# ScalarE copies the query and key banks, VectorE rotates them in SBUF: a two-layer hybrid encoder trunk

## The chip, the cores and the metric

The kernel runs on one core of one Trainium2 chip. The metric is the device time of one execution in microseconds (us), median of three runs. A core has five engines with queues of their own: TensorE (PE in the profile) multiplies matrices and writes its results to PSUM, eight banks of 128 partitions x 512 float32; VectorE (DVE), ScalarE (ACT) and GpSimd (POOL) work on elements; SyncE (SP) issues most of the loads. SBUF is the on-chip memory that all of them share. Engines wait for each other on semaphores, and each works through its own queue strictly in order.

## The reference, cut to what matters

```python
for layer in range(2):
    xn = rms_norm(x, norm_mix[layer])
    proj = xn @ w_in[layer]                     # 256 x 1024 @ 1024 x 4096
    q, k, v, u, gates = split(proj)             # q, k: 256 x (4 heads x 2 halves x 64)
    q, k = rotary(q, positions), rotary(k, positions)
    a = diff_attention(q, k, v, lam)            # softmax 1 - lam * softmax 2, per head
    s = s5_bidirectional(u, ...)                # diagonal state space, both directions
    x = x + (gate0 * (a @ w0) + gate1 * (glu(s) @ w1)) @ w_out
    x = x + (swiglu(x) if layer == 0 else top-2-of-8 experts(x))
return rms_norm(x, norm_final)

def rotary(x, positions):                       # per group of 64 columns
    x1, x2 = x[..., :32], x[..., 32:]
    return concatenate([x1 * cos - x2 * sin, x2 * cos + x1 * sin], -1)
```

All data is float32, DEPTH is 2, SEQ is 256, D_MODEL is 1024.

## The kernel before, in words

The 256 tokens stand in two halves of 128 partitions (`th` 0 and 1). Every weight matrix arrives in tiles of 128 x 2048 float32 (1 MB) in the slots of `raw`. A tile is split into two parts: ScalarE copies it rounded into `hi` (`split`, L1215), VectorE subtracts (`lo` = `raw` - `hi`, L1637, both inputs in SBUF), and TensorE multiplies hi by hi, hi by lo and lo by hi (`three`, L657). `hi` and `lo` have three slots, so tile t can be split once tile t-3 has been used.

A mixer (one per layer) first projects u, v, q and k (`W_IN_ORDER`), two tiles each: q is tiles 4 and 5, k is tiles 6 and 7. A projection writes both halves of tokens into two banks, `PJ[0]` and `PJ[1]`, 12 matmuls of 512 columns for each half and tile, and the next projection may write a bank when its reader has signalled `pj_free[th]`. u and v are read out of the banks by ScalarE (`from_pj`, L1266: a copy that multiplies by the inverse root of the norm). q and k are read by VectorE (`rotary`, L1687): for each half two products with the sine table into `areg` (L1700), one product with the cosine table in place in the bank (L1705), the sum into `qk` (L1706) and a memset that signals the bank free (L1708).

After k's projection TensorE transposes q (L675), computes the kernel of the state-space mixer inside a chunk (`inner`, L767 and L776), transposes k, and transposes the powers of the input matrix (eight turns, `B_TURNS`; ScalarE takes each out of its bank, L1253). `inner` waits for `b_part` and `kdiag_ready` from VectorE and for `c_ready` from GpSimd. The loop over eight scores and eight state-space steps follows.

The orders are written out by hand. VectorE's in the mixer of layer 0, from the sixth tile:

```python
split_static(t + 6)
rotary(l, "q", qk[:, 0, :, :])
split_static(t + 7)
input_power(b_power(3), 3)
input_power(b_power(4), 4)
# two memsets that signal b_part and b_ready
inner_diagonal(l)
rotary(l, "k", qk[:, 1, :, :])
split_static(t + 8)
split_static(t + 9)
```

In layer 1 VectorE has splits 6, then q, splits 7 and 8, then k, split 9; the input powers are GpSimd's there and are made earlier, during the feed-forward part. GpSimd in layer 0 works, in this stretch, through `c_chain` (three `product`s of 128 x 512 elements, L443 to L449, then the memset L2231 that signals `c_ready`), `phasors` (L464 to L467) and `phase_products` (L423, L2253, L2254), from which ScalarE makes the first scan table (`scan_tables`, L1326 and L1332) in the middle of the eight turns. Nearly all of these have both inputs in SBUF.

Of the kernel before, what the change touches and what calls it, by code (L numbers as in the profile page):

```python
# [18 lines left out]
P = 128  # L19
SEQ, D = 256, 1024  # L20
TH = SEQ // P
# [19 lines left out]
T_MIX = (0, T_MIX1)  # L41
# [82 lines left out]
def build(nc, x, norm_mix, w_in, attn_lambda, attn_subln, ssm_lam_re, ssm_lam_im, ssm_log_dt, ssm_b_re, ssm_b_im,  # L124
# [3 lines left out]
    ACT, ALU, AX = mybir.ActivationFunctionType, mybir.AluOpType, mybir.AxisListType  # L128
    MUL, ADD, SUB = ALU.mult, ALU.add, ALU.subtract
    ctx = ExitStack()  # L130
    with ctx:
# [3 lines left out]
        def sem(name):  # L135
            return ctx.enter_context(nc.semaphore(name))
# [10 lines left out]
        qk = sb("qk", [P, 2, TH, WA])  # L147
# [6 lines left out]
        small = sb("small", [P, 128])  # L154
# [15 lines left out]
        ident = cst[:, C_ID:C_ID + P]  # L170
# [53 lines left out]
        PJ, PY, PV, TR = banks[0:2], banks[2:4], banks[4:6], banks[6:8]  # L224

        raw_full = [sem(f"raw_full{i}") for i in range(RAWS)]
        hi_ready, lo_ready, tile_used = sem("hi_ready"), sem("lo_ready"), sem("tile_used")
        loads, x_in = sem("loads"), sem("x_in")
        rows_in, lam_in = sem("rows_in"), sem("lam_in")
# [8 lines left out]
        pj0_full = sem("pj0_full")  # L238
        pj_free = [sem("pj_free0"), sem("pj_free1")]
        dve_own, pool_own, act_own = sem("dve_own"), sem("pool_own"), sem("act_own")  # L240
        act_par, dve_par = sem("act_par"), sem("dve_par")
        rot_ready = sem("rot_ready")
# [56 lines left out]
        SS, VAR, RT, RI, MX, NB, RS, RR, C1 = 0, 2, 4, 6, 8, 10, 12, 14, 16  # L299
# [3 lines left out]
        def col(i, n=1):  # L303
            return small[:, i:i + n]
# [50 lines left out]
        def place_of(l, name):  # L355

            return W_IN_ORDER[l].index(name)

        def loop_tile(l):

            return T_MIX[l] + 16 - len(LOOP_PROJ[l])
# [6 lines left out]
        def use(l, i):  # L368

            return PJ_PER_LAYER * l + i  # L370

        def pj_read(l, i):

            return (PJ_PER_LAYER - 2) * l + i + 1
# [24 lines left out]
        place = vreg[:, 1, 0:256].rearrange("p (t s) -> p t s", t=2)  # L399
        dskip = small[:, 96:128].rearrange("p (l q) -> p l q", l=2)  # L400
        zero_mark = small[:, 92:93]
        root_mark = small[:, 22:23]
        ht_rows_hi = ht_hi[:, :, :].rearrange("p f s -> p (f s)").rearrange("p (f s) -> p f s", s=P)
        ht_rows_lo = ht_lo[:, :, :].rearrange("p f s -> p (f s)").rearrange("p (f s) -> p f s", s=P)
        gate_t = gate_store[:, :].rearrange("p (t c) -> p t c", t=TH)
# [2 lines left out]
        dve_mark, power_mark, bank_mark = small[:, 20:21], small[:, 21:22], small[:, 18:19]  # L408
# [799 lines left out]
        def _(act):  # L1208
            own = Order(act, act_own)
# [11 lines left out]
            def split_static(t):  # L1221
                s = raw_slot(t)
                split(t, raw_full[s], 32 * (raw_uses(s, t) + 1), raw[:, s, :], t % SPLITS, t >= SPLITS)
# [97 lines left out]
            def scan_tables(l, m):  # L1321
# [10 lines left out]
                    last = act.activation(lower, upper[:, :, ::-1], ACT.Copy, scale=1.0 if r == 0 else -1.0)  # L1332
                last.then_inc(wtab_ready, 1)

            def gate_block(l, name, tile, between=None):

                g, n = divmod(int(name[1]), 2)
                from_pj(l, place_of(l, name), tile, lambda th: gates[:, th, g, n * 512:(n + 1) * 512], ACT.Tanh,
                        lambda th: col(RH + th), between=between)

            def mixer(l):
# [40 lines left out]
                for g in range(2):  # L1382
                    evac((l, "u", g), ut4[:, 8 * g:8 * g + 8, :].rearrange("p q c -> p (q c)"))
                split_static(t + 6)
                split_static(t + 7)
                split_static(t + 8)
                for i in range(t + 9, loop_tile(l) + 2):
                    split_static(i)
                for th in range(TH):
# [12 lines left out]
                for s in range(8):  # L1402
# [12 lines left out]
                    if s == 7:  # L1415
                        tile, i, half = loop_proj(l, s)
                        gate_block(l, W_IN_ORDER[l][i], tile, lambda: (head_back(l, 6), weights_back(l, 7)))
                    elif s in LOOP_PROJ[l] and loop_proj(l, s)[2] == 1:
                        tile, i, half = loop_proj(l, s)
# [190 lines left out]
            for n in range(2):  # L1610
                for th in range(TH):
# [4 lines left out]
                    if n == 1:  # L1616
# [3 lines left out]
                                       scale=1.0 / D).then_inc(tail_root, 1)  # L1620
# [10 lines left out]
        def _(dve):  # L1631
            own = Order(dve, dve_own)
# [52 lines left out]
                    at_part(l, kind, 2 * th + n, 4 * n, 4, th * P, scale)  # L1685

            def rotary(l, name, dst):  # L1687
                i = place_of(l, name)

                cos_t = cst[:, C_COS:C_COS + HD].rearrange("p (t c) -> p t c", t=2)  # L1690
                sin_t = cst[:, C_SIN:C_SIN + P].rearrange("p (t c) -> p t c", t=2)
                for th in range(TH):
                    if th == 0:
                        dve.wait_ge(pj0_full, use(l, i) + 1)
                    else:
                        dve.wait_ge(tile_used, T_MIX[l] + 2 * i + 2)
                    src = PJ[th][:, :]
                    crossed = a_flat[:, 512 * th:512 * th + 512]
                    for a in range(2):
                        m = stt(crossed.rearrange("p (h a c) -> p h a c", a=2, c=32)[:, :, a, :],  # L1700
                                src.rearrange("p (h a c) -> p h a c", a=2, c=32)[:, :, 1 - a, :], col(RI + th),
                                sin_t[:, th, 32 * a:32 * (a + 1)].unsqueeze(1).broadcast_to([P, 8, 32]), MUL, MUL)
                    own.step(m)
                    halves = src.rearrange("p (h c) -> p h c", c=32)
                    own.step(stt(halves, halves, col(RI + th), cos_t[:, th, :].unsqueeze(1).broadcast_to([P, 16, 32]), MUL, MUL))  # L1705
                    tt(dst[:, th, :], src, crossed, ADD).then_inc(rot_ready, 1)  # L1706
                    dve.wait_ge(rot_ready, 4 * l + (0 if name == "q" else 2) + th + 1)
                    dve.memset(bank_mark, 0.0).then_inc(pj_free[th], 1)  # L1708

            def rotated(l, m):  # L1710

# [479 lines left out]
            for i, bank in enumerate(comb_banks):  # L2191
                n, th = i // 2, i % 2
# [228 lines left out]
```

## Time and profile before

| what | value |
|---|---|
| median of three runs | 1412.39 us (1411.92 to 1412.68) |
| the profiled execution's own time | 1413.66 us |
| its span, first to last instruction | 1410.4 us |
| TensorE busy | 1372.8 us (97% of the span) |
| VectorE busy | 1103.8 us (78%) |
| ScalarE busy | 895.5 us (63%) |
| GpSimd busy | 362.8 us (26%) |

Busy time is summed over a whole span that has very different stages: two mixers of about 250 and 190 us, a dense feed-forward part and the experts. The parts that the change touches lie at 60 to 90 us (layer 0) and 455 to 485 us (layer 1). Starts are given in us from the span's start, durations in us. Matmuls overlap each other, so their spacing (start to start) says more than their duration.

### The profile page before, as it was taken

What the parts mean: (1) busy time and instruction counts of PE and PEld (TensorE: products, weight loads), DVE (VectorE), ACT (ScalarE), POOL (GpSimd) and SP (SyncE); (2) the same over time, 40 slices, a digit from 0 to 9 for tenths busy, and PEclk for the clock granted to TensorE, in tenths of its full rate; (3) what the DMA queues carried; (4) which work ended last, traced back from release to release, by engine and by line L of the source; (5) the groups of instructions that cost most, each with busy time, mean ns of one, the idle gap of its engine ahead of it and who ended that gap; (6) DMA issues with size and microseconds to landing.
All of it is one profiled execution on the core that took longest, in us unless ns stands there. A gap on an engine that the chain in (4) does not pass through costs nothing.

```text
span 1410.4 us, 23374 instructions
## 1 busy us (share of the span) xinstructions
PE 1372.8 (97%) x8481; PEld 1123.9 (80%) x8481; DVE 1103.8 (78%) x1024; ACT 895.5 (63%) x905; POOL 362.8 (26%) x467
## 2 busy tenths in 40 slices
PE   6989999999999999999999999999999999999996
PEld 4778777888888788788888888888888888888885
DVE  6887677655455577678888888888888888898886
ACT  5445646444445455556777777777777777777775
POOL 6989709995000187000000000000000000000100
PEclk9999999999999999999999999999999999999999
DMA  9433355665555242697999999999999999999991
GB/s 244 160 121 116 116 169 166 208 197 189 184 174 180 71 156 91 243 327 282 371 370 369 389 374 379 387 359 387 384 367 389 376 376 386 367 385 350 385 349 30
DMA packets 194803, 385.12 MB, mean 273 GB/s; under 512 B 17969, under 2 KB 57265, under 8 KB 194610
## 3 DMA queue, kind: packets, MB, share of 16 engines
q1 hardware_dynamic: 188256, 367.48, 73.0%
q0 software_dynamic: 4336, 14.17, 3.9%
q10 hardware_dynamic: 2146, 2.59, 0.6%
q8 instruction: 42, 0.69, 0.2%
q14 instruction: 23, 0.19, 0.0%
HBM read 375.80 MB, written 7.34 MB: 272 GB/s over the span
## 4 chain that ended last, share of the span: by engine, by line
PE 88%; DVE 5%; ACT 3%; issue 2%; POOL 1%; DMA 0%; ACTq 0%; DVEq 0%; POOLq 0%
PE bank L657 84%; DVE lo L1637 2%; ACT hi L1215 1%; PE bank L1109 1%; PE bank L675 1%; PE bank L776 1%; POOL raw L2272 1%; PE bank L1092 0%; DVE raw L1756 0%; DVE bank L1758 0%; PE bank L983 0%; ACT at_hi L1544 0%; DMA areg<-in_norm_mix_dram 0%; PE bank L814 0%; ACT raw L1308 0%
## 5 line engine op out<-in xcount | busy, mean ns | idle before, releaser
L1637 DVE TENSOR_TENSOR lo<-raw,hi 128x2048 fp32r<-128x2048 f32 x347 | 802.5, 2324 | 156.1 <-ACT hi L1215 155.4
L1215 ACT ACTIVATE hi<-raw 128x2048 fp32r<-128x2048 f32 x347 | 663.7, 1916 | 181.5 <-PE bank L657 172.8
L657 PE MATMUL bank<-hi,at_hi 128*128 128x512 f32 x1288 | 513.9, 399 | 11.2 <-DVE lo L1637 5.8
L657 PE MATMUL bank<-hi,at_lo 128*128 128x512 f32 x1288 | 504.1, 391 | 0.0
L657 PE MATMUL bank<-lo,at_hi 128*128 128x512 f32 x1288 | 503.2, 391 | 0.0
L657 PEld LDWEIGHTS bank<-hi,at_hi 128*128 128x128 f32 x1288 | 242.9, 189 | 65.7 <-DVE lo L1637 10.8
L657 PEld LDWEIGHTS bank<-hi,at_lo 128*128 128x128 f32 x1288 | 242.6, 188 | 52.2
L657 PEld LDWEIGHTS bank<-lo,at_hi 128*128 128x128 f32 x1288 | 243.0, 189 | 47.5
L657 PE MATMUL bank<-hi,ht_hi 128*128 128x512 f32 x432 | 168.8, 391 | 0.9 <-DVE ht_lo L2115 0.9
L657 PE MATMUL bank<-hi,ht_lo 128*128 128x512 f32 x432 | 168.2, 389 | 0.0
L657 PE MATMUL bank<-lo,ht_hi 128*128 128x512 f32 x432 | 168.1, 389 | 0.0
L2348 POOL TENSOR_TENSOR small<-cst 128x1 f32<-128x1 f32 x14 | 5.9, 424 | 590.7 <-DVE slot_row L2152 298.6
L657 PEld LDWEIGHTS bank<-hi,ht_hi 128*128 128x128 f32 x432 | 81.1, 188 | 19.2 <-DVE lo L1637 1.5
L657 PEld LDWEIGHTS bank<-hi,ht_lo 128*128 128x128 f32 x432 | 81.1, 188 | 17.0
L657 PEld LDWEIGHTS bank<-lo,ht_hi 128*128 128x128 f32 x432 | 81.1, 188 | 16.6
L1553 ACT ACTIVATE ht_hi<-bank 128x512 fp32r<-128x512 f32 (+1 forms) x48 | 26.8, 559 | 55.7 <-PE bank L1109 55.7
L2272 POOL TENSOR_TENSOR raw<-raw 128x256 f32<-128x256 f32 x64 | 46.8, 761 | 22.3 <-ACT raw L1332 8.6
L1549 ACT ACTIVATE vreg<-bank 128x512 f32<-128x512 f32 (+1 forms) x48 | 27.1, 565 | 25.1 <-PE bank L657 25.1
L657 PEld LDWEIGHTS bank<-raw 64*64 64x64 f32 x1152 | 36.1, 134 | 8.0 <-issue 3.7
L657 PE MATMUL bank<-raw 64*64 64x64 f32 x1152 | 40.5, 221 | 0.3 <-POOL raw L2279 0.2
L2265 POOL MEMSET raw<- 128x4 f32 x4 | 0.3, 104 | 152.0 <-DVE raw L1733 152.0
L1227 ACT ACTIVATE at_hi<-bank 128x512 fp32r<-128x512 f32 x32 | 17.7, 596 | 33.5 <-PE bank L675 33.5
(308 smaller groups left out, 1152.7 us busy)
## 6 DMA issues: line engine op xcount, KB each, us to landing
raw<-in_moe_w_dram SPq DMA_DIRECT2D x528, 512.0 KB, 6.8
raw<-in_ffn_w_dram SPq DMA_DIRECT2D x66, 512.0 KB, 4.2
raw<-in_w_in_dram SPq DMA_DIRECT2D x64, 512.0 KB, 4.7
raw<-in_w_branch_dram SPq DMA_DIRECT2D x16, 512.0 KB, 4.5
raw<-in_w_out_dram SPq DMA_DIRECT2D x16, 512.0 KB, 4.7
raw<-in_w_glu_dram SPq DMA_DIRECT2D x4, 512.0 KB, 4.2
moe_sum<-xres POOLq DMA_DIRECT2D x3, 512.0 KB, 5.4
xres<-in_x_dram SPq DMA_DIRECT2D x2, 512.0 KB, 6.4
```

What stands on the lines that cost most here:

```text
L657: return pe.matmul(o, a, b, start=start, stop=stop)
L675: last = pe.transpose(bank[:, i * rows:(i + 1) * rows], src, ident[0:rows, 0:rows])
L776: m = pe.matmul(bank[r0:r0 + GC, c0:c0 + 64], bbar[rows, r, q, d, :], cblk[rows, r, q, 4 * d:4 * d + 4, :].rearrange("p i h -> p (i h)"), ...
L1109: m = pe.transpose(TR[0][:, f * P:(f + 1) * P], v_flat[:, f * P:(f + 1) * P], ident)
L1215: act.activation(hi[:, slot, :], src, ACT.Copy).then_inc(hi_ready, 1)
L1227: act.activation(at_hi[:, k0:k0 + kn, c0:c0 + P], bank[:, 0:kn * P].rearrange("p (k c) -> p k c", k=kn), ACT.Copy, scale=scale).then_inc(a ...
L1549: act.activation(v_flat[:, 0:h_width(c)], PJ[0][:, 0:h_width(c)], ACT.Silu).then_inc(g_ready, 1)
L1553: act.activation(ht_rows_hi[:, 0:h_width(c) // P, :], TR[0][:, 0:h_width(c)].rearrange("p (f s) -> p f s", s=P), ACT.Copy).then_inc(ht_hi_ ...
L1637: tt(lo[:, slot, :], src, hi[:, slot, :].bitcast(f32), SUB).then_inc(lo_ready, 1)
L2265: pool.memset(edge[:, :, :, 0:1], 0.0)
L2272: last = tt(dst, src[:, :, :, d, :], w[:, r:r + 1, :, d, :].broadcast_to([P, 2, 2, 64]), MUL)
L2348: tt(small[:, 82 + i:83 + i], ident[:, 0:1], ident[:, 0:1], MUL).then_inc(pool_passed, 1)
```

## The change

ScalarE gets `keep_rows`: for each half it copies the bank of q (or k), times the inverse root, into `qk`, signals `pj_free`, waits for that signal itself, and marks with a one-column activation that the rows are kept (`rows_kept`). VectorE's `rotary` waits for `rows_kept`, reads `qk` in place of the bank, uses `tensor_tensor` in place of `scalar_tensor_tensor`, and no longer signals the bank. `keep_rows` of q stands in ScalarE's queue after split 6, that of k after split 8.

```diff
+            def keep_rows(l, name, dst):
+
+                i = place_of(l, name)
+                for th in range(TH):
+                    if th == 0:
+                        act.wait_ge(pj0_full, use(l, i) + 1)
+                    else:
+                        act.wait_ge(tile_used, T_MIX[l] + 2 * i + 2)
+                    act.activation(dst[:, th, :], PJ[th][:, :], ACT.Copy, scale=inverse(th)).then_inc(pj_free[th], 1)
+                    act.wait_ge(pj_free[th], pj_read(l, i))
+                    act.activation(rows_mark, ident[:, 0:1], ACT.Copy).then_inc(rows_kept, 1)
...
                 split_static(t + 6)
+                keep_rows(l, "q", qk[:, 0, :, :])
                 split_static(t + 7)
                 split_static(t + 8)
+                keep_rows(l, "k", qk[:, 1, :, :])
...
             def rotary(l, name, dst):
-                i = place_of(l, name)
-
                 cos_t = cst[:, C_COS:C_COS + HD].rearrange("p (t c) -> p t c", t=2)
                 sin_t = cst[:, C_SIN:C_SIN + P].rearrange("p (t c) -> p t c", t=2)
                 for th in range(TH):
-                    if th == 0:
-                        dve.wait_ge(pj0_full, use(l, i) + 1)
-                    else:
-                        dve.wait_ge(tile_used, T_MIX[l] + 2 * i + 2)
-                    src = PJ[th][:, :]
+                    n = 4 * l + (0 if name == "q" else 2) + th + 1
+                    dve.wait_ge(rows_kept, n)
+                    src = dst[:, th, :]
                     crossed = a_flat[:, 512 * th:512 * th + 512]
                     for a in range(2):
-                        m = stt(crossed.rearrange("p (h a c) -> p h a c", a=2, c=32)[:, :, a, :],
-                                src.rearrange("p (h a c) -> p h a c", a=2, c=32)[:, :, 1 - a, :], col(RI + th),
-                                sin_t[:, th, 32 * a:32 * (a + 1)].unsqueeze(1).broadcast_to([P, 8, 32]), MUL, MUL)
+                        m = tt(crossed.rearrange("p (h a c) -> p h a c", a=2, c=32)[:, :, a, :],
+                               src.rearrange("p (h a c) -> p h a c", a=2, c=32)[:, :, 1 - a, :],
+                               sin_t[:, th, 32 * a:32 * (a + 1)].unsqueeze(1).broadcast_to([P, 8, 32]), MUL)
                     own.step(m)
-                    halves = src.rearrange("p (h c) -> p h c", c=32)
-                    own.step(stt(halves, halves, col(RI + th), cos_t[:, th, :].unsqueeze(1).broadcast_to([P, 16, 32]), MUL, MUL))
-                    tt(dst[:, th, :], src, crossed, ADD).then_inc(rot_ready, 1)
-                    dve.wait_ge(rot_ready, 4 * l + (0 if name == "q" else 2) + th + 1)
-                    dve.memset(bank_mark, 0.0).then_inc(pj_free[th], 1)
+                    parts = src.rearrange("p (h c) -> p h c", c=32)
+                    own.step(tt(parts, parts, cos_t[:, th, :].unsqueeze(1).broadcast_to([P, 16, 32]), MUL))
+                    tt(src, src, crossed, ADD).then_inc(rot_ready, 1)
```

## Rows read from the trace of the kernel before

**Rows 1.** The page: busy time of TensorE, and the last chain's shares by engine.
```profile
PE 1372.8 (97%) x8481; PEld 1123.9 (80%) x8481; DVE 1103.8 (78%) x1024; ACT 895.5 (63%) x905; POOL 362.8 (26%) x467
PE 88%; DVE 5%; ACT 3%; issue 2%; POOL 1%; DMA 0%; ACTq 0%; DVEq 0%; POOLq 0%
```

**Rows 2.** The chain of waits, 20 to 110 us: start, duration, what.
```profile
57.82 5.75 PE bank L657 x24
...
65.31 0.69 DVE qk L1706
...
68.59 1.28 DVE raw L1756 x2
...
76.64 0.44 DVE raw L1770
...
83.31 0.61 ACT qk L1476
...
84.05 8.68 PE bank L657 x288
```

**Rows 3.** VectorE in order of time, layer 0 (rotary halves, split 7).
```profile
63.60 0.88 DVE L1700 SCALAR_TENSOR_TENSOR areg<-bank,small,cst 128x256 f32<-128x256 f32 x2 [0.20 <-PE bank L657]
...
66.04 2.63 DVE L1637 TENSOR_TENSOR lo<-raw,hi 128x2048 fp32r<-128x2048 f32 x1
...
81.24 0.69 DVE L1706 TENSOR_TENSOR qk<-bank,areg 128x512 f32<-128x512 f32 x1
```

**Rows 4.** The chain of waits, 430 to 500 us, its longest piece.
```profile
430.00 39.41 PE bank L657 x291
```

**Rows 5.** ScalarE in order of time, layer 0.
```profile
49.20 0.69 ACT L1266 ACTIVATE vreg<-bank,small 128x512 f32<-128x512 f32 x1 [0.18 <-PE bank L657]
...
88.83 0.50 ACT L1332 ACTIVATE raw<-raw 128x128 f32<-128x128 f32 x2
...
94.67 0.21 ACT L1401 ACTIVATE small<-small 128x4 f32<-128x4 f32 x1
```

**Rows 6.** GpSimd in order of time: products beside VectorE's splits 5 and 6.
```profile
54.56 1.06 POOL L443 TENSOR_TENSOR raw<-raw,par 128x512 f32<-128x512 f32 x1
55.58 3.11 POOL L445 TENSOR_TENSOR raw<-raw,par 128x512 f32<-128x512 f32 x1
58.65 3.11 POOL L445 TENSOR_TENSOR raw<-raw,par 128x512 f32<-128x512 f32 x1
```

**Rows 7.** VectorE in order of time: splits 5 and 6 together, then split 6.
```profile
54.92 5.92 DVE L1637 TENSOR_TENSOR lo<-raw,hi 128x2048 fp32r<-128x2048 f32 x2
57.69 3.15 DVE L1637 TENSOR_TENSOR lo<-raw,hi 128x2048 fp32r<-128x2048 f32 x1
```

**Rows 8.** Groups of VectorE, 450 to 485 us (GpSimd idle): count, busy, mean ns.
```profile
L1637 DVE TENSOR_TENSOR lo<-raw,hi 128x2048 fp32r<-128x2048 f32 x4 | 9.1, 2288 | 5.3 <-ACT hi L1215 5.3
L1700 DVE SCALAR_TENSOR_TENSOR areg<-bank,small,cst 128x256 f32<-128x256 f32 x8 | 3.5, 480 | 5.5 <-PE bank L657 5.5
L1706 DVE TENSOR_TENSOR qk<-bank,areg 128x512 f32<-128x512 f32 x4 | 2.8, 692 | 0.1
```

**Rows 9.** Short instructions side by side: GpSimd, then VectorE.
```profile
28.85 0.77 POOL L2297 TENSOR_TENSOR gates<-gates 128x256 f32<-128x256 f32 x1
29.05 0.71 DVE L1997 TENSOR_TENSOR gates<-gates 64x128 f32<-64x128 f32 x1
```

**Rows 10.** GpSimd in order of time: beside rotary q, `c_ready`, the first phase table.
```profile
61.84 1.29 POOL L448 TENSOR_TENSOR raw<-raw 128x512 f32<-128x512 f32 x1
...
73.31 0.10 POOL L2231 MEMSET small<- 128x1 f32 x1
...
88.15 0.45 POOL L2254 TENSOR_TENSOR raw<-php_last 128x128 f32<-128x128 f32 x1
```

**Rows 11.** TensorE in order of time: after a pause; layer 1 around tiles 6 and 7.
```profile
33.64 0.47 PE L657 MATMUL bank<-hi,at_hi 128*128 128x512 f32 x1 [2.16 <-ACT ureg L1266]
...
35.07 0.63 PE L657 MATMUL bank<-hi,at_lo 128*128 128x512 f32 x1
...
458.26 0.47 PE L657 MATMUL bank<-hi,at_hi 128*128 128x512 f32 x1
...
463.81 0.39 PE L657 MATMUL bank<-hi,at_hi 128*128 128x512 f32 x1
```

**Rows 12.** TensorE by stretch: busy (count), granted clock, DMA share, GB/s.
```profile
36.00:38.00 2.00, 2.00 (x6) 0.50 1.04 370
```

More of the change, by code:

```diff
@@ L226, in build @@
         raw_full = [sem(f"raw_full{i}") for i in range(RAWS)]
+        rows_kept = sem("rows_kept")
         hi_ready, lo_ready, tile_used = sem("hi_ready"), sem("lo_ready"), sem("tile_used")
@@ L401, in build @@
         zero_mark = small[:, 92:93]
-        root_mark = small[:, 22:23]
+        root_mark, rows_mark = small[:, 22:23], small[:, 18:19]
         ht_rows_hi = ht_hi[:, :, :].rearrange("p f s -> p (f s)").rearrange("p (f s) -> p f s", s=P)
```

## The prediction

> **What bounds the kernel now.** I read the page's shares first: TensorE is busy 97% of the span and makes 88% of the chain that ended last [rows 1]. So a change to VectorE and ScalarE matters only where that chain leaves TensorE, and I went to the chain of waits at the two places that the diff touches.
>
> Layer 1 first, since it is simple: from 430 to 469.4 us the chain is one piece of TensorE [rows 4]. It is never left for a rotation there, and GpSimd is idle in that stretch. The rotations cost nothing today as long as they end in time.
>
> Layer 0 is different [rows 2]. TensorE's tile 5 ends at 63.57; from there the chain is on VectorE: the second half of q's rotation (last instruction 65.31 to 66.00), split 7, the input powers (68.59 on), the diagonal (76.64), and only at 77.33 TensorE's inner kernel. It ends at about 82.6; k's transposes, ScalarE's copy of them at 83.31 and the eight turns from 84.05 follow. In this stretch TensorE waits for VectorE, and a microsecond more on VectorE is a microsecond more on the run. k's rotation (81.24 to 81.93, [rows 3]) ends 0.7 us before k's transposes start: hardly any slack.
>
> **The third engine.** GpSimd's and VectorE's rows in one stretch show what the diff's words do not. GpSimd's products of 128x512 take 1.06 us [rows 6]; the two beside splits 5 and 6 took 3.11 each. The split takes 2.29 us when GpSimd is idle [rows 8], but here two took 5.92 and the second 3.15 [rows 7]. The ends fit one pattern. Product L443 ends at 55.62; 55.49 + 2.29 is 57.78, split 5's end. Product L445 ends at 58.69 = 57.63 + 1.06; 58.55 + 2.29 = 60.84, split 6's end. The next product ends at 61.76 = 60.70 + 1.06. So they take turns, one instruction each, every one starting 0.14 us before the recorded end of the other's. It holds for short ones too: a GpSimd product ends at 28.85 + 0.77 = 29.62, and VectorE's L1997 of 64x128, asked for at 29.05, ends at 29.76 [rows 9]. Counted back from there by the 0.28 us that its kind takes, it started at 29.48, again 0.14 before the product's end. VectorE instructions with one input in PSUM show none of this: L1700 has 0.88 for two beside busy GpSimd [rows 3] as in layer 1 (0.48 each, [rows 8]), and GpSimd's L448 beside them its plain 1.29 [rows 10].
>
> The change turns 16 such instructions with a PSUM input (four per half, four halves per mixer) into instructions with both inputs in SBUF. In layer 0 GpSimd is busy all through them.
>
> The Trainium skill (SBUF — State Buffer, Who interferes with whom) speaks against the change in the same way: a VectorE instruction with two SBUF inputs and a GpSimd instruction that reads SBUF exclude each other, and who issues first holds the port for the whole instruction. The rows agree but for the 0.14 us of overlap; taken literally it is a rival below.
>
> **Layer 0, step by step.** (1) Handoff. The ScalarE copy of a bank with a scale takes 0.69, the mark 0.21 [rows 5], waits 0.04 each: 0.98. It cannot be hidden for the second half, whose bank is full at 63.56. VectorE may start half 0 at 61.84 (before: 60.88), half 1 not before 64.54. The mark is bounded by 0.10 (a one-column memset, [rows 10]) and 0.50 (two activations of 128 columns, [rows 5]).
>
> (2) The rotation itself, without GpSimd: two sine products of 0.43 (0.05 less than the 0.48 of today), cosine and sum 0.69 each (as L1706) and waits: 2.25 a half, today 2.43. I see no faster form: 2288 ns for 2048 against 692 for 512 [rows 8] is 1.04 ns an element with SBUF inputs only, just what the PSUM ones have.
>
> (3) Taking turns with GpSimd, q. From 61.84 the products are L448, L449 (1.29 each), then L443, L443, L445, L445 (1.06), L448, L449. With each start at the other's end less 0.14: L448 to 63.13; sine 62.99-63.42; L449 to 64.57; sine 64.43-64.86; L443 to 65.78; cosine 65.64-66.33; L443 to 67.25; sum 67.11-67.80. Half 1: L445 to 68.72; sine to 69.01; L445 to 69.93; sine to 70.22; L448 to 71.37; cosine to 71.92; L449 to 73.07; sum 72.93-73.62. Today it ends at 66.00: +7.6. If VectorE wins the first turn (both ask at 61.84) every step comes one product earlier, 72.4: +6.4. With an overlap of 0.10 in place of 0.14 it is 74.2: +8.2.
>
> GpSimd loses little by it, since split 7 now falls later: `c_ready` comes at 73.2, as today (73.31, [rows 10]), long before it is needed.
>
> (4) Split 7 waits 0.3 for a product and ends at 76.27 (68.67 today). TensorE, which wants tile 7 at about 69.0, idles 7.3 us. That is not added: the inner kernel waits for VectorE anyway. From split 7's end to the diagonal's end VectorE needs 8.4 us as today (68.67 to 77.08): 84.70. +7.6, TensorE's inner kernel at 84.96.
>
> The pause has a clock price. After 2.16 us of idling at 31.5 us matmuls came 0.43 apart from 34.65 to 38.06 in place of 0.23, granted clock 0.50 (1.2 of 2.4 GHz) [rows 11, 12]: 8 of them, 1.6 us. Tile 7, from 76.32, needs 5.46 + about 1.9 and the q transposes 1.0 to 1.9: 84.7 to 85.6. Hidden, or 0.6 late.
>
> (5) k's rotation, from 84.72: the phase products (0.40 and 0.45 us) stand between now, 0.2 for each: 90.24, 5.5 us against 4.8. ScalarE's split 9 and q's copies come after the kept k (84.7 to 87.7), ahead of k's transposes. These start at 90.28 (the inner kernel ends at 90.26), the two inner copies of ScalarE, which wait for the rotation, end at 91.26, and k's copy starts at 91.26 in place of 83.31: **+7.95**. The first phase table (88.60 today, 88.3 then) and splits 8 and 9 (95.1) are early for what follows; everything behind is moved by the same amount, since loads and GpSimd's steps of the loop wait for this chain too.
>
> **Layer 1.** GpSimd is idle. ScalarE's split 7 (452.93 today) now stands behind the kept q, whose second half is full at 458.28: kept and marked 459.27, rotation to 461.5, VectorE's split 7 to 463.85. Tile 7 was taken at 463.81; tile 6 starts 0.2 sooner, because its bank is free at 456.3 and the pause before 458.26 goes [rows 11]. TensorE then waits some 0.3, net **+0.15** (bounds -0.22 and +0.5). k's rotation ends at 472.6, wanted at 475.
>
> **Sum.** 7.95 + 0.15 = 8.1 us. Against the profiled execution: 1413.66 + 8.1 = 1421.8 (span 1418.5). Its own time stands 1.27 above the median of the runs, so for the median 1412.39 + 8.1 = **1420.5**.
>
> **Rivals.**
> (a) VectorE has the right of way: its instructions are not held up, only GpSimd's. Then VectorE is 0.8 later, but GpSimd loses 2 x (0.29 + 0.55) = 1.7 per half, 6.7 over four halves, and the first phase table comes at 95.3, where ScalarE would take it at 88.83 + 0.8 [rows 5, 10] and holds back the turns behind it: +6.5. 1412.4 + 6.5 + 0.15 = 1419.0. For it: GpSimd lost most beside splits. Against: split 6's 3.15.
> (b) The port is held for the whole instruction, no overlap. The same walk with 0.14 set to 0 ends k's rotation at 94.7: +12.6, 1425.0. Against: three ends in [rows 6, 7].
> (c) Short instructions do not collide. What is left is the handoff: 0.8 (half 1 of q ends at 66.80) and 0.15: 1413.3. Against: [rows 9].
> (d) Not slower: with the banks left sooner and instructions from SBUF cheap, q's second half is done by 66.0 despite the handoff, and tile 6 of layer 1 starts 0.22 sooner: 1412.2. It decides at whether a half takes under 1.5 us (today 2.43) and split 7 of layer 1 lands before 463.58. Against: the 1.04 ns an element. Even then the gain is 0.2 us: VectorE's relief elsewhere is under TensorE's cover.
>
> **How the numbers follow.** Taking turns 0.64 (own range 1418.0 to 1422.5, from first turn and overlap), (a) 0.12, (b) 0.06, (c) 0.12, (d) 0.03, others 0.03. Under 2.8 us (0.2%) counts as no change: (c) and most of (d), 0.13; faster 0.02; slower 0.85. Range 1414.5 to 1425.5: it holds the forecast, (a) and (b).
>
> **What would show it.** Right: L1637 of tile 7 at about 74 instead of 66; the four `qk`/`areg` groups of VectorE in layer 0 with means well over 0.43 and 0.69 (0.9 to 1.5) and in layer 1 with exactly these; a TensorE pause of 7 us before tile 7 at 69 us with granted clock 0.5 behind it; `inner` at 85; L1476 of k at 91. Wrong: means equal in both layers, GpSimd's L443 to L449 longer instead (rival a), or the pause under 1 us (c).

## The result, and the profile after

The changed kernel takes 1419.22 us (median of 5 runs, 1418.98 to 1420.38) beside 1411.92 for the kernel before on the same chip (5 runs, 1410.74 to 1412.68): ratio 1.0054, interval 1.0043 to 1.0065. That is 7.3 us slower (interval 6.1 to 9.2). The profiled execution took 1419.51 with a span of 1417.0 us, against 1413.66 and 1410.4; TensorE's mean granted clock is 0.993 against 0.995.

Line numbers moved a little: a split is now L1652 (L1637 before), the matmuls L658 (L657), the rotation's sine, cosine and sum L1711, L1716 and L1717, the kept copy L1344 and its mark L1346, the copies of turned heads L1491 (L1476).

The page: busy time by engine. TensorE's busy time is 1.5 us longer than in [rows 1]; VectorE's 5.8, ScalarE's 6.4 and GpSimd's 4.7 us.

```profile
PE 1374.3 (97%) x8481; PEld 1124.3 (79%) x8481; DVE 1109.6 (78%) x1016; ACT 901.9 (64%) x921; POOL 367.5 (26%) x467
```

These sums and the chain's shares (TensorE 89% in place of 88%) hardly move. The chain of waits in layer 0 shows the loss (start, duration, what; "issue" is time in which the engine waited for nothing that the profile shows; compare [rows 2]). It leaves TensorE at 60.93 instead of 63.57, and stays on ScalarE and VectorE for 14.8 us. The copy L1344 and its mark are the handoff:

```profile
60.96 0.70 ACT qk L1344
...
61.91 1.86 DVE areg L1711 x2
...
72.47 3.28 DVE lo L1652
...
75.79 8.52 PE bank L658 x24
...
88.89 1.14 issue
...
91.50 0.61 ACT qk L1491
...
92.24 8.68 PE bank L658 x288
```

The last line stood at 84.05 before [rows 2]: +8.19 at that point. Now the two engines side by side while q is rotated (start, duration, operation; in brackets the idle time before it and what ended it). VectorE, to be compared with [rows 3]:

```profile
61.91 1.85 DVE L1711 TENSOR_TENSOR areg<-qk,cst 128x256 f32<-128x256 f32 x2 [1.00 <-ACT small L1346]
63.80 1.67 DVE L1716 TENSOR_TENSOR qk<-qk,cst 128x512 f32<-128x512 f32 x1
65.50 1.43 DVE L1717 TENSOR_TENSOR qk<-qk,areg 128x512 f32<-128x512 f32 x1
66.86 2.48 DVE L1711 TENSOR_TENSOR areg<-qk,cst 128x256 f32<-128x256 f32 x2
...
70.84 1.64 DVE L1717 TENSOR_TENSOR qk<-qk,areg 128x512 f32<-128x512 f32 x1
72.39 3.34 DVE L1652 TENSOR_TENSOR lo<-raw,hi 128x2048 fp32r<-128x2048 f32 x1
```

GpSimd, to be compared with [rows 10]:

```profile
61.91 1.57 POOL L449 TENSOR_TENSOR raw<-raw 128x512 f32<-128x512 f32 x1
63.45 1.47 POOL L450 TENSOR_TENSOR raw<-raw 128x512 f32<-128x512 f32 x1
65.00 2.86 POOL L444 TENSOR_TENSOR raw<-raw,par 128x512 f32<-128x512 f32 x2
...
73.65 0.10 POOL L2240 MEMSET small<- 128x1 f32 x1
73.71 2.53 POOL L465 TENSOR_TENSOR raw<-raw,php_last 128x256 f32<-128x256 f32 x1
...
87.60 0.64 POOL L2263 TENSOR_TENSOR raw<-php_last 128x128 f32<-128x128 f32 x1
```

Read the two together. GpSimd's first product ends at 63.48. The sine product in front of it ends at 61.91 + 0.43 = 62.34; less 0.14 is 62.20, and the product's plain 1.29 from there gives 63.49. VectorE's second sine product then starts at 63.48 - 0.14 = 63.34 and ends at 63.77, where the row has it (61.91 + 1.85 = 63.76). Each engine goes through one instruction while the other waits. VectorE, whose instructions are the shorter ones, loses most. Carried on in this way from 61.91, with 0.14 at each change of turn and the plain durations, the walk gives every end in the two lists down to split 7 to within 0.1 us. q's rotation takes 10.6 us, from 61.91 to 72.48; before it ended at 66.00. In the end split 7, held for the last product, ends at 75.73. GpSimd's next 128x256 product, held for split 7, ends at 76.24 = 75.73 - 0.14 + 0.64 (rounding aside), 0.64 being what its twin L466 takes right behind it.

TensorE waits for that split, and starts again at half clock (TensorE in order of time, then all engines by stretch: busy and count of TensorE, its weight loads, VectorE, ScalarE and GpSimd, then the granted clock, DMA share, GB/s; [rows 11, 12] have the shorter pause of before):

```profile
75.79 0.79 PE L658 MATMUL bank<-hi,at_hi 128*128 128x512 f32 x1 [6.72 <-DVE lo L1652]
...
84.16 1.03 PE L676 MATMUL bank<-cst,qk 128*128 128x128 f32 x8
85.12 0.30 PE L768 MATMUL bank<-raw,cst 16*16 16x64 f32 x8
```

```profile
77.00:81.00 4.00, 4.00 (x11) 3.12 (x10) 3.93 (x9) 0.00 (x0) 3.77 (x8) 0.50 0.72 253
```

Matmuls from 76.39 to 81.51 come 0.43 apart in place of 0.23, granted clock 0.50 (1.2 of 2.4 GHz), and tile 7 takes 8.4 us. VectorE's diagonal ends at 84.16, and before, TensorE's inner kernel began 0.25 after that. Here it begins at 85.12, so it waits for TensorE's own tile and the q transposes behind it: 0.7 us is the clock's. The inner kernel starts 7.79 later than before, and the pause at "issue" inside it is 1.14 in place of 0.74: together the 8.19.

In layer 1, where GpSimd is idle, the same instructions have the plain price of [rows 8] (groups of VectorE, 455 to 500 us: count, busy, mean ns; the sine products take 422 where those from the bank had 480, and the cosine's L1716 has 692):

```profile
L1711 DVE TENSOR_TENSOR areg<-qk,cst 128x256 f32<-128x256 f32 x8 | 3.0, 422 | 7.4 <-ACT small L1346 7.4
L1717 DVE TENSOR_TENSOR qk<-qk,areg 128x512 f32<-128x512 f32 x4 | 2.8, 693 | 0.1
```

TensorE is 8.09 later than before at layer 1's tile 4, 8.02 later at its tile 7 and 8.16 later at its inner kernel (478.38 against 470.22), so in these two executions the change adds 0.07 us there. The span grows by less, 6.6 us: from layer 1's inner kernel to the start of its scores the profiled execution of before loses 1.7 us more than that of after. The chain of waits shows two pauses at "issue", 0.11 and 0.89 us after, 0.25 and 1.43 us before, and the stretches behind them have different clocks: the eight turns take 10.3 us before and 9.3 after. By stretch, before:

```profile
478.00:482.00 4.00, 3.95 (x82) 3.98 (x84) 0.00 (x0) 1.46 (x3) 0.00 (x0) 0.57 0.23 42
```

and after:

```profile
486.00:490.00 4.00, 3.81 (x128) 3.68 (x126) 0.00 (x0) 1.87 (x4) 0.00 (x0) 1.00 0.22 39
```

The experiments show the same: half clock behind a wait of about two microseconds comes in some executions and not in others. So one profile of each kernel is good for where the time goes, and the medians for how much.

### The profile page after: what moved, and what is told of

Same layout as the page of the kernel before. It is cut to its first block, busy times and chain, and to the rows that moved or that the text cites. A ratio compares the mean times of both kernels' runs of the same rounds, so it can differ in the third digit from the quotient of the medians.

```text
span 1417.0 us, 23382 instructions
## 1 busy us (share of the span) xinstructions
PE 1374.3 (97%) x8481; PEld 1124.3 (79%) x8481; DVE 1109.6 (78%) x1016; ACT 901.9 (64%) x921; POOL 367.5 (26%) x467
## 4 chain that ended last, share of the span: by engine, by line
PE 89%; DVE 5%; ACT 3%; issue 2%; DMA 0%; POOL 0%; ACTq 0%; DVEq 0%; POOLq 0%
PE bank L658 85%; DVE lo L1652 2%; ACT hi L1216 1%; PE bank L1110 1%; PE bank L676 1%; PE bank L777 1%; PE bank L1093 0%; PE bank L815 0%; PE bank L984 0%; DMA areg<-in_norm_mix_dram 0%; ACT at_hi L1559 0%; DVE areg L1711 0%; ACT raw L1309 0%; DVE qk L1716 0%; DVE qk L1717 0%
## 5 line engine op out<-in xcount | busy, mean ns | idle before, releaser
L1652 DVE TENSOR_TENSOR lo<-raw,hi 128x2048 fp32r<-128x2048 f32 x347 | 803.1, 2326 | 155.9 <-ACT hi L1216 155.4
L658 PE MATMUL bank<-hi,at_hi 128*128 128x512 f32 x1288 | 515.5, 400 | 18.2 <-DVE lo L1652 12.5
L658 PE MATMUL bank<-hi,at_lo 128*128 128x512 f32 x1288 | 504.8, 392 | 0.0
L658 PE MATMUL bank<-lo,at_hi 128*128 128x512 f32 x1288 | 504.1, 391 | 0.0
L658 PEld LDWEIGHTS bank<-hi,at_hi 128*128 128x128 f32 x1288 | 243.4, 189 | 73.2 <-DVE lo L1652 18.3
L658 PEld LDWEIGHTS bank<-hi,at_lo 128*128 128x128 f32 x1288 | 243.1, 189 | 52.8
L658 PEld LDWEIGHTS bank<-lo,at_hi 128*128 128x128 f32 x1288 | 243.7, 189 | 47.6
L658 PE MATMUL bank<-hi,ht_hi 128*128 128x512 f32 x432 | 168.8, 391 | 0.9 <-DVE ht_lo L2124 0.9
L658 PE MATMUL bank<-hi,ht_lo 128*128 128x512 f32 x432 | 168.1, 389 | 0.0
L658 PE MATMUL bank<-lo,ht_hi 128*128 128x512 f32 x432 | 168.1, 389 | 0.0
L658 PEld LDWEIGHTS bank<-hi,ht_hi 128*128 128x128 f32 x432 | 81.1, 188 | 19.2 <-DVE lo L1652 1.5
L658 PEld LDWEIGHTS bank<-hi,ht_lo 128*128 128x128 f32 x432 | 81.1, 188 | 17.0
L658 PEld LDWEIGHTS bank<-lo,ht_hi 128*128 128x128 f32 x432 | 81.1, 188 | 16.6
L658 PEld LDWEIGHTS bank<-raw 64*64 64x64 f32 x1152 | 36.1, 134 | 7.7 <-issue 3.7
L658 PE MATMUL bank<-raw 64*64 64x64 f32 x1152 | 40.5, 221 | 0.1
```

What stands on the lines that cost most here:

```text
L658: return pe.matmul(o, a, b, start=start, stop=stop)
L1652: tt(lo[:, slot, :], src, hi[:, slot, :].bitcast(f32), SUB).then_inc(lo_ready, 1)
```

## The experiments

All times are medians beside the kernel before on the same chip (1411.38 for the first three, 1411.63 for the next four, 1411.41 for the last two; 21 or 22 runs each). "Loop" is the start of layer 0's scores on TensorE in the profiled execution, 93.46 before and 101.65 after. It holds differences that have nothing to do with the rotations: tile 5 starts between 57.13 (TensorE kept busy) and 58.37 (halved products), at 57.82 before and 57.91 after.

| kernel | median us (runs) | ratio, interval | span | loop |
|---|---|---|---|---|
| change in layer 1 alone | 1411.33 (11) | 0.9998, 0.9989 to 1.0007 | 1409.9 | 94.01 |
| change in layer 0 alone | 1419.35 (5) | 1.0053, 1.0039 to 1.0067 | 1415.7 | 100.47 |
| rotation from the bank | 1413.75 (11) | 1.0017, 1.0008 to 1.0026 | 1411.3 | 95.04 |
| GpSimd quiet | 1411.38 (11) | 0.9997, 0.9988 to 1.0006 | 1409.4 | 93.52 |
| halved products | 1418.19 (6) | 1.0049, 1.0037 to 1.0061 | 1415.9 | 100.54 |
| TensorE kept busy | 1418.17 (5) | 1.0047, 1.0033 to 1.0060 | 1415.5 | 100.54 |
| q rotated late | 1412.00 (12) | 1.0004, 0.9995 to 1.0013 | 1409.7 | 93.17 |
| q rotated late, split 9 later | 1414.48 (11) | 1.0017, 1.0008 to 1.0026 | 1412.0 | 93.98 |
| k of layer 0 alone | 1413.44 (11) | 1.0013, 1.0004 to 1.0022 | 1411.9 | 95.73 |

### Where: one layer at a time

```diff
-                keep_rows(l, "q", qk[:, 0, :, :])
+                if l == 1:
+                    keep_rows(l, "q", qk[:, 0, :, :])
...
-                    rotary(l, "q", qk[:, 0, :, :])
+                    (rotary if l == 1 else rotary_bank)(l, "q", qk[:, 0, :, :])
```

`rotary_bank` is the rotation of before; k likewise. The second kernel has `l == 0` in these places.

> ScalarE keeps the rows and VectorE rotates from SBUF in layer 1 alone; layer 0 rotates from the banks as before. Theory (VectorE and GpSimd take turns at SBUF, in layer 0 only, where GpSimd is busy): time as before, 1412.1 (+0.15), between 1411.6 and 1412.6; rotation instructions 0.38 to 0.43 and 0.69 us. Rival 1 (the handoff through ScalarE is the cost, the same in both layers): half of the 7.3 us, 1415.6. Rival 2 (ScalarE's later split 7 holds up TensorE): 1413 to 1415 with a TensorE pause before tile 7.

> The change in layer 0 alone. Theory: all of the difference, 1419 to 1420; VectorE's q rotation 61.9 to 72.5, k's 5.4 us, tile 7 on TensorE at 75.8 with granted clock 0.5. Rival (handoff, both layers alike): 1415.6.

Layer 1 alone costs nothing that can be measured, and layer 0 alone carries all of it. The first median lies just below the 1411.6 to 1412.6 of the theory, the second within its 1419 to 1420. The handoff is in both layers; a busy GpSimd only in layer 0. VectorE's q rotation in the second kernel repeats the one of after to within 0.01 us in each duration. It starts 0.55 sooner: this execution has a granted clock of 1.00 from 34 to 38 us, where after has 0.50 and then 0.67 and before 0.66 and then 0.50 [rows 12].

### What: the same handoff, the source left in the bank

```diff
-                    act.activation(dst[:, th, :], PJ[th][:, :], ACT.Copy, scale=inverse(th)).then_inc(pj_free[th], 1)
+                    act.activation(PJ[th][:, :], PJ[th][:, :], ACT.Copy, scale=inverse(th)).then_inc(bank_scaled, 1)
...
-                    src = dst[:, th, :]
+                    src = PJ[th][:, :]
...
-                    tt(src, src, crossed, ADD).then_inc(rot_ready, 1)
+                    tt(dst[:, th, :], src, crossed, ADD).then_inc(rot_ready, 1)
+                    dve.wait_ge(rot_ready, n)
+                    dve.memset(bank_mark, 0.0).then_inc(pj_free[th], 1)
```

> The handoff stays in both layers (ScalarE multiplies the bank by the inverse root in place, marks, VectorE waits for the mark and rotates with tensor_tensor), but the rows stay in the bank, so three of VectorE's four instructions of a half have one SBUF input, as has the sum. Theory (the second SBUF input is the cost): layer 0 later by the handoff only, 0.8 us, layer 1 0.15 to 0.5: 1412.8 to 1413.5; rotation instructions 0.43 and 0.69 in both layers, GpSimd's products 1.06 and 1.29. Rival (the wait for ScalarE and its moved split 7 are the cost): 1419.

VectorE in order of time, with GpSimd at work beside it all the while (its products 1.29, 1.26 and 1.04 us each):

```profile
61.58 0.75 DVE L1711 TENSOR_TENSOR areg<-bank,cst 128x256 f32<-128x256 f32 x2 [0.97 <-ACT small L1346]
62.37 0.70 DVE L1716 TENSOR_TENSOR bank<-bank,cst 128x512 f32<-128x512 f32 x1
63.10 0.69 DVE L1717 TENSOR_TENSOR qk<-bank,areg 128x512 f32<-128x512 f32 x1
```

With one input of the pair in PSUM, 1.67 becomes 0.70 and 1.43 becomes 0.69, and GpSimd has its plain price too. The handoff alone moved the inner kernel from 77.33 to 78.22, by 0.9 where 0.8 was expected. The whole cost 2.4 us (interval 1.1 to 3.7), and 1413.75 lies above the 1412.8 to 1413.5 of the theory, far from the rival's 1419. Two reasons show. TensorE's wait for the diagonal grew from 1.74 to 2.07 us, and the inner kernel behind it ran at half clock (by stretch):

```profile
79.00:80.00 1.00, 1.00 (x50) 1.00 (x42) 0.97 (x2) 0.00 (x0) 1.00 (x2) 0.50 0.00 0
```

Its first 128 matmuls took 3.58 us in place of 1.98. The pause of 0.74 that before has inside this stage is not there, so the stage is 0.70 longer in all, and the scores of layer 0 start 1.58 later than before, not 0.9. And layer 1's inner kernel is 2.41 later, another 0.8: TensorE waits 0.73 us before tile 6 for VectorE's signal that the bank is free, which here comes only after handoff and rotation. So what the prediction counted as "the handoff alone" had about the right size at its place and missed what follows from it.

### Why: GpSimd out of the way

```diff
-                for k in range(1, 4):
+                for k in range(1, 2 if l == 0 else 4):
                     product(tt, own, c_power(k), c_power(k - 1), 32 * l, A_RE, A_IM, pt, True)
+                if l == 0:
+                    for k in (2, 3):
+                        for part in c_power(k)[0][2]:
+                            last = pool.memset(part, 0.0)
+                    own.step(last)
                 mark(c_ready)
+                if l == 0:
+                    pool.wait_ge(rot_ready, 2)
```

> The changed kernel, with GpSimd out of the way of q's rotation in layer 0: the last two of its three c_chain products are left out (four memsets stand for them, so the state-space output of layer 0 is not the reference's), and then GpSimd waits for the end of q's rotation. Theory (turns at SBUF): q's rotation ends at 66.8 in place of 72.5, its instructions 0.4 and 0.69 us; split 7 ends at about 69.3, no long TensorE pause and no clock of 0.5; k's rotation still meets phasors and phase products (5 to 6 us): 1413 to 1414. Rival (handoff or queue order of ScalarE, GpSimd no matter): stays at 1419.

VectorE, then GpSimd:

```profile
61.46 0.76 DVE L1711 TENSOR_TENSOR areg<-qk,cst 128x256 f32<-128x256 f32 x2 [1.87 <-ACT small L1346]
62.26 0.69 DVE L1716 TENSOR_TENSOR qk<-qk,cst 128x512 f32<-128x512 f32 x1
...
66.31 2.28 DVE L1652 TENSOR_TENSOR lo<-raw,hi 128x2048 fp32r<-128x2048 f32 x1
```

```profile
66.47 2.62 POOL L465 TENSOR_TENSOR raw<-raw,php_last 128x256 f32<-128x256 f32 x1 [10.70 <-DVE qk L1717]
```

Everything of the change is in place but GpSimd's products, and the loss is gone. That it came out at the level of before, and not 1.4 to 2.4 us above as expected, has its reason in the rows. The products are missing beside VectorE's splits 5 and 6 too, which take 4.49 us together in place of 5.92 [rows 7], so tile 5 starts at 57.45 in place of 57.82 and hides half of the handoff. q's rotation ends at 66.39 (66.00 before), 0.39 late, and split 7 takes 2.28 instead of 2.63 [rows 3], 0.35 less, because GpSimd leaves it alone as well. These two gains belong to the missing products and not to the change; without them the handoff would show. k's rotation still takes 5.4 us, since GpSimd works again by then, and costs nothing: it ends at 82.47, and the scores start at 93.52 (93.46 before). TensorE's wait before the inner kernel is 2.01 us here, about as long as in the kernel above, and this execution kept the full clock behind it:

```profile
77.00:79.00 2.00, 1.71 (x115) 1.63 (x118) 1.90 (x5) 1.15 (x3) 1.92 (x4) 1.00 0.00 0
```

### How: shorter instructions, shorter turns

```diff
+                    power = c_power(k)[0][2]
+                    halves = [(q, q + 8, [a[:, q:q + 8] for a in power]) for q in (0, 8)]
-                    product(tt, own, c_power(k), c_power(k - 1), 32 * l, A_RE, A_IM, pt, True)
+                    product(tt, own, halves if l == 0 else c_power(k), c_power(k - 1), 32 * l, A_RE, A_IM, pt, True)
```

> The changed kernel, with each instruction of GpSimd's c_chain of layer 0 cut into two of 128x256 elements: same work, twice the instructions. If the two engines take turns by whole instructions, a VectorE instruction waits for at most 0.6 us in place of 1.1 to 1.3: q's rotation takes 6 to 8 us in place of 10.6 and ends near 70, the run is 2 to 3 us shorter than the changed kernel: 1416 to 1417.5, if c_ready (more and shorter instructions, later by 1 to 2 us) doesn't become the wait. Rival (the port is shared by bandwidth, not by instruction): q's rotation as long as before, 10 us or more, 1419.

GpSimd's instructions have half the size, their sum is the same or more. If a turn lasts one instruction, VectorE waits less.

```profile
62.39 1.23 DVE L1711 TENSOR_TENSOR areg<-qk,cst 128x256 f32<-128x256 f32 x2 [1.46 <-ACT small L1346]
63.65 0.99 DVE L1716 TENSOR_TENSOR qk<-qk,cst 128x512 f32<-128x512 f32 x1
```

The rotation takes 7.4 us (62.39 to 69.75) in place of 10.6, and the inner kernel starts at 81.15, 4.0 sooner than in after. The cosine product's 0.99 is its own 0.69 and a GpSimd product of 0.60 less 0.28, as in after 1.43 was 0.69 and 1.06 less 0.28, each to within 0.04. But the run is not clearly faster than after (1418.19, ratio 1.0049, against 1.0054, the intervals overlap), and outside the 1416 to 1417.5 expected: GpSimd's `c_ready` comes at 79.31 instead of 73.65, and its first phase table so late that TensorE's turns wait 1.99 us for ScalarE's copies behind it and VectorE, at 97.21, 3.20 us for the scan table. ScalarE's row for that table:

```profile
96.67 0.51 ACT L1333 ACTIVATE raw<-raw 128x128 f32<-128x128 f32 x2 [2.87 <-POOL raw L2265]
```

The scores start at 100.54. The mechanism held; the time of the whole was taken by a wait that the expectation left out.

### The clock's part: no pause before tile 7

```diff
                     proj(t + 2 * i, l, i, 0, True, False)
+                    if l == 0 and i == 3:
+                        bank = open_turn((l, "q", 0))
+                        for _ in range(7):
+                            mm(bank[:, 0:448], ident, ident[:, 0:1].broadcast_to([P, 448]), True, True)
                     proj(t + 2 * i + 1, l, i, 4, False, True)
```

> The changed kernel, with seven matmuls of no use between tiles 6 and 7 of layer 0, where TensorE paused for 6.7 us. If the clock of 0.5 behind the pause is part of the cost, tile 7 takes 5.5 us in place of 8.4 and the inner kernel starts when VectorE's diagonal is done (84.4 in place of 85.1): 0.7 us shorter, 1418.5. Rival (hidden under VectorE's chain): no change, 1419.2.

```profile
68.15 5.45 PE L658 MATMUL bank<-cst 128*128 128x448 f32 x14
75.03 0.50 PE L658 MATMUL bank<-hi,at_hi 128*128 128x512 f32 x1 [1.44 <-DVE lo L1656]
...
83.66 0.30 PE L768 MATMUL bank<-raw,cst 16*16 16x64 f32 x8 [1.99 <-DVE raw L1783]
83.89 3.55 PE L777 MATMUL bank<-raw 64*16 64x64 f32 x128
```

Useless matmuls fill all but 1.44 us of the pause, tile 7 takes 5.6 us instead of 8.4, and the inner kernel starts 0.25 after VectorE's diagonal (83.41), as it did before: the 0.7 us is indeed the clock's. The medians (1.0047 and 1.0054) don't tell this kernel from after. In the profiled execution the clock took its price one step later: TensorE now ends tile 7 early, waits 1.99 us for the diagonal, and the inner kernel behind that wait gets half clock.

```profile
85.00:86.00 1.00, 1.00 (x49) 1.00 (x41) 0.97 (x3) 0.00 (x0) 1.00 (x2) 0.50 0.00 0
```

While VectorE is the late one, an idle stretch of TensorE must stand somewhere, and filling one moved it to the next.

### k of layer 0 alone

```diff
-                keep_rows(l, "q", qk[:, 0, :, :])
...
-                keep_rows(l, "k", qk[:, 1, :, :])
+                if l == 0:
+                    keep_rows(l, "k", qk[:, 1, :, :])
```

> The change for k of layer 0 alone: ScalarE keeps k's rows, VectorE rotates them from SBUF; q and layer 1 rotate from the banks. GpSimd runs short instructions there (0.3 to 0.7 us) and not the 1.1 to 1.3 us products beside q. Theory (a turn costs what the other engine's instruction lasts): k's rotation takes 5.3 to 5.6 us in place of 4.8, the run is 0.5 to 0.8 us longer than before: 1412 to 1412.5, so q's rotation carries over 6 of the 7.3 us. Rival (each rotation costs half): 1415.

```profile
76.67 2.39 DVE L1734 TENSOR_TENSOR areg<-qk,cst 128x256 f32<-128x256 f32 x2
79.10 1.10 DVE L1739 TENSOR_TENSOR qk<-qk,cst 128x512 f32<-128x512 f32 x1
```

The kernel is 2.0 us slower than before (interval 0.6 to 3.1), more than expected. With q left as it was, k's rotation falls 7.5 us sooner, and meets GpSimd's 128x512 products L465 and L466 (1.17 and 1.25 us beside it) where in after it meets products of 128x128. It takes 7.0 us, not 5.4, and TensorE's k transposes, at 83.73, wait 1.26 us for it. What a rotation costs depends on which of GpSimd's instructions it meets. The transposes start 1.12 later than before, the scores 2.27: the rest is half clock behind the wait (TensorE in order of time, where the same group took 2.08 before, then by stretch):

```profile
85.36 3.03 PE L658 MATMUL bank<-cst,raw 64*64 64x64 f32 x64
```

```profile
84.00:86.00 2.00, 2.00 (x20) 1.67 (x20) 2.00 (x2) 1.75 (x4) 2.00 (x1) 0.52 0.00 0
```

So this kernel does not give k's share of the loss in after, where k's rotation meets short products and takes 0.6 us more than before. There 7.8 of the 8.2 us were in place when the inner kernel started, behind q's rotation, the split held up with it and the clock.

### Versions meant to win

The first keeps the change for q of layer 0 only, and moves it: the bank is kept as in after, but VectorE rotates q after the diagonal, when GpSimd's long products are over; the q transposes go behind the inner kernel, k's turns behind the others. In ScalarE's queue the first scan table, which stood in the middle of the eight turns, and k's copies now stand behind all eight.

```diff
-                    rotary(l, "q", qk[:, 0, :, :])
                     split_static(t + 7)
...
                     inner_diagonal(l)
-                    rotary(l, "k", qk[:, 1, :, :])
+                    rotary(l, "q", qk[:, 0, :, :])
+                    rotary_bank(l, "k", qk[:, 1, :, :])
...
                     evac((l, "b", g), bflat[:, g * 512:(g + 1) * 512])
-                    if g == 1:
+                    if l > 0 and g == 1:
                         scan_tables(l, 0)
...
+                if l == 0:
+                    scan_tables(l, 0)
+                    for th in range(TH):
+                        evac_heads(l, "k", th, k_t)
```

> A version meant to beat both: in layer 0 ScalarE copies q's rows out so that the bank is free early, and VectorE does split 7, the input powers and the diagonal first, then q's rotation (from SBUF) and k's (from the bank); TensorE transposes k after the eight turns. Layer 1 as before. If VectorE's chain 63.6 to 77.3 is what TensorE waits for, the inner kernel starts at about 74.6 in place of 77.33 and the loop some 2 us earlier: 1409.5 to 1410.5. Rival (c_ready, GpSimd delayed by the new overlaps, or the first scan table becomes the wait): 1411 to 1413.

The inner kernel starts at 74.24, 3.1 sooner than before, and nothing of it is left at the end: 1412.00, the rival's range. Before, the first phase table ended at 88.60 [rows 10] and GpSimd's copy in front of its products with the splits stood here:

```profile
81.89 0.24 POOL L487 COPY raw<-php_last 128x64 f32<-128x64 f32 x1
```

GpSimd in this kernel:

```profile
83.78 2.34 POOL L489 COPY raw<-php_last 128x64 f32<-128x64 f32 x1
...
90.10 0.45 POOL L2300 TENSOR_TENSOR raw<-php_last 128x128 f32<-128x128 f32 x1
```

A copy of 128x64 that takes 0.24 alone takes 2.34 beside split 8. But the two splits hold GpSimd no longer than they did before: from that copy to the end of the first two L425 products it takes 5.10 us, and 5.05 before. What makes the phase table late, 90.55 in place of 88.60, is already there at the copy (83.78 against 81.89), and comes from the `phasors`, which now take turns with q's rotation (the second 128x128 product of them took 0.90 there, 0.46 before). Even so the table is not what VectorE's state rotation waits 3.58 us for. The chain of waits goes from TensorE to ScalarE's copy of the eighth turn and its scan table behind it:

```profile
90.54 0.60 ACT raw L1261
...
91.87 0.70 DVE raw L1766
```

And k's transposes, now behind the turns, wait with the scores for ScalarE's copies, which stand behind the scan table:

```profile
93.17 0.67 PE L659 MATMUL bank<-qk,ureg 64*128 64x256 f32 x2 [1.32 <-ACT qk L1505]
```

From the last of the turns to the scores TensorE takes 2.7 us in place of 0.7, and a pause of 0.58 at "issue" within the turns is new: of the 3.1 us, 0.3 are left at the scores (93.17 against 93.46). So the reading on which the next expectation rests, that the splits held GpSimd up, is not what the rows show. The second version puts split 9 behind the first row maximum, to spare GpSimd that turn, and makes the first scan table two turns earlier than the first version did.

```diff
                 for s in range(8):
                     row_max(l, s)
+                    if l == 0 and s == 0:
+                        split_static(t + 9)
```

> The version with the late rotation, mended where its trace showed the gain go: there the inner kernel started 3.1 us sooner than before (74.24), but splits 8 and 9 held GpSimd up for 4 us, so that the first phase table, the scan table and VectorE's first rotated() came at 91.9 (before: 89.4). Here VectorE does split 9 behind the first row_max and ScalarE makes the first scan table two turns earlier. If GpSimd was the wait: first phase table near 88.5, rotated() at 90, the first s5_out near 100.3 (before 101.4): 1410.5 to 1411.3. Rival (another wait of the loop takes its place): 1411.5 to 1412.5.

The chain of waits:

```profile
96.39 0.69 DVE small L1823
97.08 2.25 DVE lo L1667
99.33 0.62 DVE small L1920
...
108.31 4.19 POOL raw L2320 x3
```

The first phase table ends at 89.04, 1.5 us sooner than in the first version. VectorE's state rotation starts at 91.14, only 0.7 sooner, because ScalarE makes the scan table behind its copy of the sixth turn, at 90.31. And split 9 now stands between the row maximum and the softmax, on the chain. By the medians this kernel is 3.1 us slower than before (interval 1.1 to 3.7), worse than theory and rival had it. Neither version beats the kernel before. Late rotation with the scan table left where it was has not been run.

## Why the prediction was right, point by point

1420.5 was forecast, in 1414.5 to 1425.5; 1419.22 was measured. The sum was 8.1 us and the medians differ by 7.3. By its steps:

| step | predicted | measured |
|---|---|---|
| q's rotation starts | 61.84 | 61.91 |
| q's rotation ends | 73.62 (72.4 if VectorE has the first turn) | 72.48 |
| split 7 ends | 76.27 | 75.73 |
| diagonal ends | 84.70 | 84.16 |
| inner kernel starts | 84.96 | 85.12 |
| k's rotation ends | 90.24 | 89.59 |
| k's copy starts | 91.26 | 91.50 |
| layer 1 | +0.15 | +0.07 at the inner kernel |

- **Taking turns, each start 0.14 before the other's end.** Right, and shown from three sides: source in the bank, GpSimd quiet, products halved. By the Trainium skill (SBUF — State Buffer, Who interferes with whom) the port is held for the whole instruction; the rows agree that a turn is one whole instruction, and again have the next one start 0.14 us before the end.
- **The first turn.** Both engines asked at 61.91, and VectorE won. The working had GpSimd first and named the other order as 72.4; it was that. Its 1.1 us shrank to 0.54 at split 7, which met the last product at its start and was held about 1.0 us instead of 0.3.
- **The clock, "hidden, or 0.6 late".** It was late, by 0.7. The estimate took 1.9 us more for tile 7; it was 2.9 (8.4 against 5.46), since the half clock lasted 5.7 us and not the 3.4 of [rows 11, 12]. With the first turn this nearly cancels: that the inner kernel is 0.16 from its forecast is in part luck.
- **k's rotation.** 5.4 us against 5.5. It was not the last to arrive: the inner kernel ended at 90.87, after it, with a pause of 1.14 at "issue" that the sum had at the 0.74 of before. The forecast had k's copy wait for the rotation, through ScalarE's two inner copies; the second of these waited for TensorE's inner kernel instead. The rotation ended 0.65 sooner than forecast and the inner kernel 0.61 later, so here too 91.50 against 91.26 is partly luck.
- **Layer 1.** +0.15 was forecast, with a wait of 0.3 before tile 7. The wait is 0.18, the inner kernel is 0.07 later in relation to tile 4, and the change in layer 1 alone gives a ratio of 0.9998 (0.9989 to 1.0007).
- **Rival (a), VectorE with the right of way,** gave 1419.0, as near to the median as the forecast: the time could not refute it, the rows do. VectorE's L1716 took 1.67 and 1.43 instead of 0.69, and the phase table came at 88.24, not at 95.3. Rival (b), no overlap, fails by the starts and the time, (c), short instructions do not collide, by the rows (the two sine products of a half took 1.85 and 2.48 in place of 0.76) and the time, (d) by all.

The difference of 0.8 us between sum and medians isn't settled. The interval, 6.1 to 9.2, holds both, and the change in layer 0 alone stands 8.0 us above its own before (interval 5.5 to 9.5). What varies by that much from one execution to the next is seen: pauses at "issue" inside layer 0's inner kernel of 0.74 (before), 1.14 (after), 1.10 (halved products), 0.95 (k alone), 0.79 (q late) and 0.78 us (GpSimd quiet), and half clock behind short waits (3.58 and 3.55 us in place of 1.98 for the inner kernel's first 128 matmuls, from the bank and with TensorE kept busy). The sum took both as they lay in one execution of before. The pauses' cause was not tried.

## What to carry to other kernels

Before moving VectorE's operands from PSUM to on-chip memory, look at what GpSimd runs in the same microseconds: if both engines have work waiting, such an instruction takes its own duration plus one whole GpSimd instruction, less 0.28 us (0.14 at each of the two changes of turn), so here 0.69 became 1.4 to 1.7 beside products of 1.06 and 1.29, and the loss fell entirely in the layer where GpSimd was busy. The count of instructions and the length of GpSimd's ones set the price, not VectorE's work; on a bank as source the two engines don't meet. Shortening the turns, or moving the work to where GpSimd is free, then needs a look at GpSimd's own deadline: here the halved products ended in a wait for its phase tables. The late rotation lost its gain elsewhere, to ScalarE's order and to transposes that had been hidden: moving an instruction moves what stands behind it.

## What the runs showed of the hardware that was not expected

- The price of a pause in TensorE isn't a constant. After 6.72 us (both executions with it, after and layer 0 alone) the granted clock was 0.50, for 5.7 us in after; after the 2.16 us of [rows 11] it was 0.50 for 3.4 us, and after 2.87 us in the kernel with halved products for 3.0. After waits of 2.07 and 1.99 us the clock fell in two kernels, after 2.01 in another and 1.74 before it did not. With k of layer 0 alone it fell to 0.52 after a wait of 1.26, which stood behind a pause of 0.95.
- GpSimd is held as hard as it holds: a copy of 128x64, 0.24 us alone, took 2.34 beside a split.
- Two engines that ask in the same hundredth of a microsecond (61.91): VectorE went first, and by the walk the order decided over 1.1 us.
